# Four PSUM banks take decays, logarithms and queries of the HGRN heads, and neighbouring heads are interlaced at their border

## What is computed

```python
def hgrn2_mix(q, f_logit, i, lb):
    f = lb + (1.0 - lb) * jax.nn.sigmoid(f_logit)
    k = 1.0 - f
    logf = jnp.log(f)
    ...
    def step(state, inp):
        qb, kb, gb, vb = inp
        b = jnp.cumsum(gb, axis=2)
        diff = b[:, :, :, None, :] - b[:, :, None, :, :]
        decay = jnp.exp(jnp.where(causal[:, :, None], diff, -jnp.inf))
        a = jnp.einsum('bhtd,bhsd,bhtsd->bhts', qb, kb, decay)
        o = (jnp.einsum('bhts,bhsv->bhtv', a, vb)
             + jnp.einsum('bhtd,bhdv->bhtv', qb * jnp.exp(b), state))
        ...
```

## Time and profile before

| | us |
|---|---|
| median of 3 runs | 3338.77 (3337.95 to 3343.27) |
| the profiled execution | 3341.62 |
| its span, first to last instruction | 3339.8 |
| PE / DVE / ACT / POOL busy in the span | 3167.4 / 1775.6 / 824.6 / 2336.8 |
| the stage of the HGRN heads, by PE's rows | 154.62 to 362.04 |

### The profile page before, as it was taken

The page is one execution under the profiler, slowest core; times in us unless marked ns, Lnnn a source line. Parts: engine busy times, 40 slices in busy tenths (PEclk is TensorE's granted clock), DMA queues, the critical chain, the costliest instruction groups (busy, mean ns, idle before and its releaser), DMA issues.

```text
span 3339.8 us, 41949 instructions
## 1 busy us (share of the span) xinstructions
PE 3167.4 (95%) x14202; PEld 2538.5 (76%) x14202; DVE 1775.6 (53%) x2584; ACT 824.6 (25%) x1390; POOL 2336.8 (70%) x1127
## 2 busy tenths in 40 slices
PE   8988999999999999999999999999999877699998
PEld 6777777788888888888888788888888654378886
DVE  6488746221246443344432466676676765676621
ACT  3233223220112332332334101010101344322211
POOL 6733554677776788878887788888888641078876
PEclk9999999999999999999999999999999987799999
DMA  4211221233323344434444666666665220023232
GB/s 142 88 39 44 87 65 63 69 94 120 107 95 108 119 172 172 173 129 158 173 170 166 212 194 183 189 188 187 190 182 169 79 63 13 7 84 99 94 94 76
DMA packets 245540, 405.62 MB, mean 121 GB/s; under 512 B 145600, under 2 KB 145728, under 8 KB 244160
## 3 DMA queue, kind: packets, MB, share of 16 engines
q1 hardware_dynamic: 224560, 331.68, 32.1%
q10 hardware_dynamic: 20880, 72.62, 5.6%
HBM read 335.04 MB, written 69.21 MB: 121 GB/s over the span
## 4 chain that ended last, share of the span: by engine, by line
PE 72%; DVE 5%; ACT 2%; issue 1%; POOL 0%; ACTq 0%; POOLq 0%; DVEq 0%
PE bank L531 22%; PE bank L533 22%; PE bank L532 22%; PE bank L832 3%; ACT hot L1056 1%; PE bank L921 1%; PE bank L931 0%; PE bank L810 0%; DVE h_lo L1578 0%; DVE bank L1566 0%; DVE sb_w L2121 0%; DVE sb_z L2125 0%; PE bank L939 0%; PE bank L946 0%; ACT act_out_stage L1292 0%
## 5 line engine op out<-in xcount | busy, mean ns | idle before, releaser
L462 POOL TENSOR_TENSOR w_hi<-w_raw,ones 128x1024 fp32r<-128x1024 f32 x494 | 960.9, 1945 | 929.0 <-PE bank L533 853.1
L464 POOL TENSOR_TENSOR w_lo<-w_raw,w_hi 128x1024 fp32r<-128x1024 f32 x494 | 1238.6, 2507 | 38.8
L531 PE MATMUL bank<-h_hi,w_hi 128*128 128x512 f32 x2176 | 867.3, 399 | 10.4 <-DVE h_lo L1578 7.1
L533 PE MATMUL bank<-h_hi,w_lo 128*128 128x512 f32 x2176 | 849.8, 391 | 0.0
L532 PE MATMUL bank<-h_lo,w_hi 128*128 128x512 f32 x2176 | 849.2, 390 | 0.0
L531 PEld LDWEIGHTS bank<-h_hi,w_hi 128*128 128x128 f32 x2176 | 410.5, 189 | 104.5 <-DVE h_lo L1578 13.9
L533 PEld LDWEIGHTS bank<-h_hi,w_lo 128*128 128x128 f32 x2176 | 409.6, 188 | 86.8
L532 PEld LDWEIGHTS bank<-h_lo,w_hi 128*128 128x128 f32 x2176 | 410.6, 189 | 83.7 <-issue 3.2
L531 PE MATMUL bank<-ew_hi,w_hi 128*128 128x512 f32 x1024 | 405.2, 396 | 3.0 <-DVE ew_lo L2033 3.0
L533 PE MATMUL bank<-ew_hi,w_lo 128*128 128x512 f32 x1024 | 405.1, 396 | 0.0
L532 PE MATMUL bank<-ew_lo,w_hi 128*128 128x512 f32 x1024 | 405.1, 396 | 0.0
(11 more groups left out here) (354 smaller groups left out, 3749.5 us busy)
## 6 DMA issues: line engine op xcount, KB each, us to landing
w_raw<-weights SPq DMA_DIRECT2D x494, 512.0 KB, 3.5
acts<-act_out_stage ACTq DMA_DIRECT2D x128, 256.0 KB, 2.8
gates<-gate_stage ACTq DMA_DIRECT2D x8, 4096.0 KB, 13.1
acts_in<-acts SPq DMA_DIRECT2D x128, 256.0 KB, 4.3
gates_in<-gates SPq DMA_DIRECT2D x128, 256.0 KB, 4.7
resid<-x SPq DMA_DIRECT2D x4, 512.0 KB, 8.1
resid<-x ACTq DMA_DIRECT2D x4, 512.0 KB, 8.1
out<-final SPq DMA_DIRECT2D x3, 512.0 KB, 2.6
```

The source lines that it names most:

```text
L462: nc.gpsimd.tensor_tensor(w_hi[:, pair, :], w_raw[:, slot, :], one_col.to_broadcast((P, 1024)), ALU.mult).then_inc(hi_split, 1)
L464: nc.gpsimd.tensor_tensor(w_lo[:, pair, :], w_raw[:, slot, :], f32(w_hi[:, pair, :]), ALU.subtract).then_inc(split_done, 1)
L531: mm(out_, hi, rhs_hi, start=first, stop=False)
L533: return mm(out_, lo, rhs_hi, start=False, stop=last)
```

## The change

PE's border between two heads is written anew. Level 0 of the next head and its first weight part come before the product of scores and values of the head just done (`hgrn_out`), and the far product behind that. ACT copies the output of head i-1 behind level 3 of head i, no longer at the end of its own head. Four idle banks become operands: the decays of levels 4 and 6 lie in bank 4 and of 5 and 7 in bank 5, the far keys' decays (all but the first head's) in bank 4, a copy of the head's logarithms in bank 6 (read by `diff` from level 5 on), and a copy of the next head's queries in bank 7 (read by `far_scaled`). The last two are new ACT copies of 512 columns per head.

```diff
+    def level_decay(l):
+        return lev_e[:, l % 2, :] if l < 4 else bank[4 + l % 2][:]
...
-        def hgrn_head(i, p):
+        def hgrn_head(i, p, after_level):
...
-            pe.wait_ge(head_ready, c.due(head_ready, 2))
+            pe.wait_ge(head_ready, c.due(head_ready, 4 if after_level else 2))
             level(head_k[p], one(hq_, i), 0)
+            pe.wait_ge(tok_read, 2 * TT)
+            tile_part(0, bank[0][:], 0)
+            if after_level:
+                after_level()
             pe.wait_ge(far_ready, c.due(far_ready))
-            pe.wait_ge(tok_read, 2 * TT)
...
-            tile_part(0, bank[0][:], 0)
             for l in range(1, len(LEVELS)):
...
-            pe.wait_ge(lev_read, c.due(lev_read, 0))
+        def hgrn_out(p, since=0):
+            pe.wait_ge(lev_read, c.due(lev_read, 0, back=since))
             pe.wait_ge(att_far, c.due(att_far, 0))
             pe.wait_ge(o_read, c.due(o_read, 1, back=1))
...
+        def head_out(i):
+            act.wait_ge(o_done, c.due(o_done))
+            fn_at(one(hq_, i), bank[6][:], ACT.Copy).then_inc(o_read, 1)
...
             for l in range(1, len(LEVELS)):
+                if l == 4:
+                    act.wait_ge(o_read, c.due(o_read, 0))
+                    fn_at(bank[6][:], one(hb, i), ACT.Copy).then_inc(head_ready, 1)
                 act.wait_ge(lev_diff, c.due(lev_diff, 2))
-                fn(lev_e[:, l % 2, :], lev_e[:, l % 2, :], ACT.Exp).then_inc(lev_exp, 1)
+                fn(level_decay(l), level_decay(l), ACT.Exp).then_inc(lev_exp, 1)
...
+                if l == 3 and not first:
+                    head_out(i - 1)
                 if l == 4 and not last:
                     head_copies(i + 1, 1 - p)
+                if l == 5 and not last:
+                    fn_at(bank[7][:], one(hq_, i + 1), ACT.Copy).then_inc(head_ready, 1)
...
-            e_left, e_right = halves(lev_e[:, l % 2, :], w)
+            e_left, e_right = halves(level_decay(l), w)
             last = left[:, :, w - 1:w].to_broadcast((P, T // (2 * w), w))
+            if l == 5:
+                dve.wait_ge(head_ready, c.due(head_ready))
+            if l > 4:
+                left, right = halves(bank[6][:], w)
...
+                if l == 3:
+                    dve.wait_ge(att_far, c.due(att_far, 3))
                 if l < top:
                     diff(i, l + 1)
                 select(l - 1)
...
+            far = bank[4][:, 0:384].rearrange("p (j n) -> p j n", n=P)
             if not last:
-                far_start(i + 1)
+                far_start(i + 1, far)
             select(top)
             if not last:
-                far_scaled(i + 1, 1 - p)
+                far_scaled(1 - p, far, bank[7][:], 3)
```

More of the change, by code:

```diff
@@ L712, in hgrn_head, with hgrn_heads @@
             ins.then_inc(o_done, 1)
-        def hgrn_heads(i):
+        def hgrn_heads(i, first=False):
             for p in range(2):
-                hgrn_head(i * 2 + p, p)
-        c.repeat(HG_HEADS // 2, hgrn_heads)
+                hgrn_head(i * 2 + p, p, None if first and p == 0 else lambda: hgrn_out(1 - p, 1))
+        c.once(hgrn_heads, 0, True)
+        c.once(hgrn_heads, 1)
+        c.loop(2, HG_HEADS // 2, hgrn_heads)
+        hgrn_out(1)
         settle()
@@ L1132, in head_copies, with far_decays @@
             fn_at(head_v[p][:], hv[:, :, bass.ds(i * 128, 128)], ACT.Copy).then_inc(head_ready, 1)
-        def far_decays(i):
+        def far_decays(i, e):
             act.wait_ge(far_e_ready, c.due(far_e_ready, 2))
-            fn(far_e[:], far_e[:], ACT.Exp).then_inc(far_q_exp, 1)
+            fn(e, e, ACT.Exp).then_inc(far_q_exp, 1)
             b = one(hb, i)
@@ L1159, in hgrn_head, with hgrn_heads @@
             if not last:
-                far_decays(i + 1)
+                far_decays(i + 1, bank[4][:, 0:384])
             act.wait_ge(tile_done, c.due(tile_done))
             fn_at(one(rk, i), bank[1][:], ACT.Copy, scale=RET_DK ** -0.5).then_inc(acc_read_act, 1)
[L1163 to L1168, removed]
+        def hgrn_heads(i, first=False, last=False):
+            hgrn_head(i * 2, 0, first)
+            hgrn_head(i * 2 + 1, 1, False, last)
         fn(head_k[0][:], hk[:, 0, :], ACT.Copy).then_inc(head_ready, 1)
         act.wait_ge(decay_done, c.due(decay_done, HG_HEADS))
-        far_decays(0)
+        far_decays(0, far_e[:].rearrange("p a n -> p (a n)"))
         evac_tm(1, hv)
@@ L1177, in _ @@
         act.wait_ge(tok_read, c.due(tok_read, TT))
-        c.once(hgrn_heads, 0)
-        c.loop(1, HG_HEADS // 2 - 1, hgrn_heads)
-        c.once(hgrn_heads, HG_HEADS // 2 - 1, True)
+        c.once(hgrn_heads, 0, True)
+        c.once(hgrn_heads, 1)
+        c.loop(2, HG_HEADS // 2 - 1, hgrn_heads)
+        c.once(hgrn_heads, HG_HEADS // 2 - 1, False, True)
+        head_out(HG_HEADS - 1)
         act.dma_start(cos_sin[:], tables[:, TAB["cos"][0]:TAB["cos"][0] + 1024].rearrange("p (a n) -> p a n", a=2)).then_inc(cs_in, 16)
@@ L1682, in far_start, with far_scaled @@
             diff(i, 2)
-        def far_scaled(i, p):
-            dve.wait_ge(head_ready, c.due(head_ready, 2))
+        def far_scaled(p, e, q, copies):
+            dve.wait_ge(head_ready, c.due(head_ready, copies))
             dve.wait_ge(far_q_exp, c.due(far_q_exp, 7))
-            q = one(hq_, i)
-            tt_(far_k[:], head_k[p][:, 0:384].rearrange("p (j n) -> p j n", n=P), far_e[:], ALU.mult).then_inc(dve_step, 1)
+            tt_(far_k[:], head_k[p][:, 0:384].rearrange("p (j n) -> p j n", n=P), e, ALU.mult).then_inc(dve_step, 1)
             tt_(far_q[:, 0:384], far_q[:, 0:384], q[:, 128:512], ALU.mult).then_inc(dve_step, 1)
@@ L1716, in hgrn_heads @@
             hgrn_head(i * 2 + 1, 1, last)
-        far_start(0)
-        far_scaled(0, 0)
+        far_start(0, far_e[:])
+        far_scaled(0, far_e[:], hq_[:, 0, :], 2)
         c.once(hgrn_heads, 0)
```

7 lines of the change are left out of this document (4 added, 3 removed).

## The result

The kernel after takes 3301.73 us (median of 4 runs, 3300.03 to 3303.89), the kernel before 3338.79 (4 runs, 3337.95 to 3343.27). The ratio is 0.9887, with an interval of [0.987, 0.9904]: 37.1 us faster. In a second series of runs it was 3304.12 against 3339.44, 0.9901 [0.9883, 0.9919], 35.3 us. The forecast of 3310 had the direction and the mechanism inside the stage of the heads right; the time is outside its range of 3306 to 3323, because more was gained than forecast.

A forecast was written before the change was run, and what follows sets the result against it. PE was taken to bound the kernel, waiting in the heads on DVE, which POOL holds. Removing all waits but the first gives 29.8 us, less 0.8 kept: 3341.62 - 29.0 = 3312.6, less 2.85 to the median, rounded 3310; range 3306 to 3323.

The forecast's parts named there:

- What held PE up: Heads' stage: PE waits 27.2 us, nearly all on DVE, whose instructions with two SBUF inputs are held while POOL reads SBUF.
- The rival that the lock persists or moves: Heads' stage: POOL still holds DVE instructions on banks, or PE waits at level 1 instead; gain 19, 3320 us; chance 0.08.
- Operands in PSUM cost nothing: DVE in the heads: 432 ns for 256 columns written to a bank against 0.43 us; no extra cost taken.
- rival 1: Widths 2 and 1: short runs in a bank cost up to 0.30 us more per instruction; gain 17, 3322 us; chance 0.12.
- the slower case: From width 4 down, twelve DVE instructions per head on banks take 1.03 us each; 20 us slower, 3359; chance 0.03.
- Rival 3: Heads' stage: fully busy PE gets clock 0.98 instead of 1.00, costing 3.6 us, 3313; forecast with this rival: chance 0.75.
- The sum inside the stage: Heads' stage: all PE waits but the start's 1.3 us go; 176.3 + 1.3 = 177.6 us, 29.8 less.
- the kept 0.8: Heads' stage: 0.8 us held back from the 29.8 gain for waits of a tenth at the tight border.
- level 0, "1.06 at most": PE's border between heads: level 0 takes at most 1.06 us of a head's 22.04 without waits.
- signs of being right: Stage 177 to 180 us, heads 22 to 22.3, PE waits 1.3 to 3, bank-input DVE instructions 0.42 to 0.45, far products 0.56.
- The 203.5 of the working: Heads' stage before: 176.3 us of PE work plus 27.2 of waits, leaving 3.9 of 207.42 for drained pipelines.
- The sum outside the stage: Later stages: PE time saved in the heads reaches the end unchanged; chance 0.02 that a later stage eats the gain.

The follow-up runs named there:

- The padding: Kernel after plus 140 matmuls with unread results behind the last head, so later stages begin as late as before: 3339.62 us; with 70 matmuls 3321.07 us.
- the shorter wait: Kernel after, but before the retention's first scores PE waits for each bank at its own product instead of for all four evictions: 3306.47 us, 0.9897 of before.
- the padded one: Kernel after with the per-bank wait before the retention's first scores and 140 unread matmuls behind the last head: 3336.78 us, 0.9991 of before.

## Why the prediction was too small

**What held PE up: right.** Differences and products with one input in a bank are not held by POOL, those with both in SBUF are, in the same kernel and at the same place. All 23 waits on DVE are gone. The rival that the lock persists or moves falls with it; the level 1 product is held at each border, as foretold, and ends 0.47 to 0.74 before it is needed. The Trainium skill's rule on who holds whom ("SBUF — State Buffer", Who interferes with whom) is what the runs show: 974 against 420 ns for the number of SBUF inputs alone.

**Operands in PSUM cost nothing: right.** 414 to 426 ns at all widths; rival 1 and the slower case, which wanted 0.73 and 0.82, are out. The 65 ns that the Trainium skill's page "VectorE: DVE Perf Modes" (errata table) would add to a PSUM source do not show here: 421 ns with the bank, 424 the least of the same products without.

**The clock in the stage: right to leave out.** It stays at 1.00. Rival 3 looked at the wrong side: not a fuller PE loses clock here, but one that has waited.

**The sum inside the stage: mis-sized by 2.3 us, and the kept 0.8 on top.** The failed term is level 0, "1.06 at most". I took the busy time of its row, where the slot to the next instruction is 0.80; over eight heads that is 2.1. With 2.16 for scores by values and 1.30 for the far product the head comes to 21.69, and 21.68 was measured. So of the signs of being right the stage of 177 to 180 (175.3) and the head of 22 to 22.3 missed, and the waits and the durations on DVE held. The 203.5 of the working then left 3.9 for drained pipelines, 0.16 for each wait, and this was the other half of the same mistake. Against the stage of after, the surplus over the named waits is 32.1 - 25.9 = 6.2 for 23 waits before, 1.9 for 7 with the far keys in SBUF and 2.2 for 8 without the copy of the logarithms: 0.27 each time. It doesn't hold for short waits: the banks alone have 1.5 for their four waits of 0.2 to 0.4. The stage gave 32.1, of which I had counted 29.8 and claimed 29.

**The sum outside the stage: the step that failed.** The prediction let the gain of the stage pass through unchanged ("PE saves here should reach the end") and gave a chance only to a later stage that eats some of it. The medians gained 37.1 and 35.3, so 5.0 and 3.2 came from later stages. The stage's 32.1 alone would have given 3306.7, just inside the range; this put the time outside it. The profiles name a part: the lower clock behind four waits took 6.8 us before and 1.7 and 3.4 after, 5.1 and 3.4 less. That these are nearly the differences of the medians is in part luck, since a profile shows one execution: the first two lie 41.6 us apart, and 4.4 of these come neither from the stage of the heads nor from this clock; the second two lie 37.7 apart, with 2.2 such. The padding speaks for it that this goes with when the stages begin and not with the edits: with the later stages back at their old times, the lower clock is back at all four places (8.5 us), and of the gain in the later stages nothing is left. Against it, the kernel with the levels in SBUF stands at the same times and had it at two places only. At the retention's start the clock stayed up in both kernels with the shorter wait; but it also did in six of eleven with the long one, so this supports the wait as the cause and does not prove it. Only the padded one tells something: it stands at 459.89, near the four that fell from 461.68 to 462.50, but 463.29 did not fall either.

What stays open is what decides whether the clock falls behind such a wait. At the retention's start it fell at 446.05, 461.68, 461.99, 462.26 and 462.50 and not at 429.99, 430.25, 431.58, 441.60, 448.79 and 463.29: neither the place in the program nor the length of the wait decides alone, and if the time of its beginning does, these eleven do not say how. It also stays open where the last 4.5 us of spread in the table come from; between the first profiles some of it lies in the experts' second layer, 717.7 against 713.3, of which the clock explains 1.7. Less the lower clock that layer takes 713.2 to 716.0 in the thirteen profiles, and neither edit nor starting time sorts them: at about 1880 us before has 716.0 and the kernel with the order only 713.2.

No kernel tried beats the one after: the shorter wait removes 1.5 us at its place and had the lower clock at four others (20, 595, 1760 and 1845 us).

## What to carry to other kernels

When DVE is late beside a busy POOL, look at how many of its inputs are in SBUF before looking at how much it does: one input moved to an idle PSUM bank, even at the price of a copy on ACT, freed it. For the full gain all the instructions under POOL had to be freed: the levels alone brought 22 of the stage's 32 us, the far keys alone none, so the halves don't add up. Cost an engine's slot from start to start in an undisturbed row, never from the busy time of a row, and then check that the price per wait that is left over is a believable one. Where PE has single waits of 2 us, an earlier start of the stage can gain or lose a few us by the clock alone; the range should hold that.

## What the runs showed of the hardware

- A wait of PE costs 0.27 us beyond its named length, in three kernels alike; in the two with lower clock in the stage the same reckoning gives 0.19 and 0.30, and 0.37 for the four short waits of the banks alone.
- Behind waits of 1.8 to 3.0 us PE's granted clock fell to 1.2 GHz for about 3.4 us in some executions and not in others, 1.7 us lost each time; at some places it lasted about twice as long and 3.4 were lost. None of the 24 waits of up to 2.1 in the stage before was followed by it, while six of eleven were with the levels in SBUF.
- The COPY_PREDICATED of 256 columns takes 0.73 under POOL's instruction as without it (240.56 lies ahead of the split), and 0.43 at greater widths; that of 0.43 at 255.06 lies wholly under POOL's first half. It is not held though its mask is in SBUF.
